# Delta net: the convolution's centre tap on ScalarE, fixed banks for projections and gate, merge chunks moved within the last head

## The reference, cut to what matters

```python
def dwconv_centred(x, w):                 # CONV_K = 4, padding 2 on the left, 1 on the right
    ...                                   # out[t] = sum over k of w[k] * x[t + k - 2], per channel
c = jax.nn.silu(dwconv_centred(qkv, conv_w))
q, k, v = jnp.split(c, [DN_QK, 2 * DN_QK], axis=-1)
q = q * rsqrt(sum(q*q) + EPS) * DN_DK ** -0.5
k = k * rsqrt(sum(k*k) + EPS)
# chunked gated delta rule, forward and backward in time:
A = where(strict, (k*beta) @ k.T * decay, 0); solve (A + I) u = v*beta, (A + I) w = k*beta*exp(gc)
v_new = u - w @ S; o = qg @ S + att @ v_new; S = S*exp(gl) + kd.T @ v_new
o = rmsnorm(o) * norm_g * silu(z)
```

## Time and profile before

| what | us |
|---|---|
| median of 3 runs (3611.55 to 3613.46) | 3612.29 |
| the profiled execution's own time | 3611.45 |
| its span in the trace | 3609.67 |
| TensorE busy (97% of the span) | 3492.7 |
| VectorE busy (52%) | 1886.8 |
| ScalarE busy (32%) | 1138.1 |
| POOL busy (24%) | 869.6 |

### The profile page before, as it was taken

How to read it: one execution, slowest core, us unless ns; L and a number is a source line. 1 busy time by engine, 2 the same in 40 slices (tenths; PEclk the granted TensorE clock), 3 DMA queues, 4 the chain that set the end, 5 groups by cost and what they waited for, 6 DMA issues and landing times.

```text
span 3609.7 us, 53450 instructions
## 1 busy us (share of the span) xinstructions
PE 3492.7 (97%) x22170; PEld 2304.4 (64%) x22170; DVE 1886.8 (52%) x3502; ACT 1138.1 (32%) x2145; POOL 869.6 (24%) x704
## 2 busy tenths in 40 slices
PE   7999999999999999999999999999999999999998
PEld 4555555665668876676666656444555545878887
DVE  3555553355445353666666653455777732554543
ACT  3443443222232022333333322764544521110100
POOL 2212121222210003444444410223445420000000
PEclk9999999999999999999999999999999999999999
DMA  5121111111102111111111111221101011322221
GB/s 227 65 79 70 56 65 47 35 35 47 35 36 105 71 65 59 48 48 39 45 48 48 54 71 59 83 76 62 48 31 48 16 64 62 112 83 81 87 81 56
DMA packets 29551, 229.73 MB, mean 64 GB/s; under 512 B 3072, under 2 KB 6784, under 8 KB 9728
## 3 DMA queue, kind: packets, MB, share of 16 engines
q1 hardware_dynamic: 29312, 226.33, 17.0%
HBM read 224.22 MB, written 2.10 MB: 63 GB/s over the span
## 4 chain that ended last, share of the span: by engine, by line
PE 88%; DVE 6%; ACT 3%; issue 1%; DMA 1%; POOL 0%; SPq 0%; DVEq 0%; ACTq 0%; POOLq 0%
PE bank L1284 12%; PE bank L1610 8%; PE bank L1503 7%; PE bank L1951 7%; PE bank L1606 4%; PE bank L1978 4%; PE bank L1730 3%; PE bank L1569 3%; PE bank L1869 2%; PE bank L1409 2%; PE bank L1689 2%; PE bank L1696 2%; PE bank L1442 2%; PE bank L1231 2%; PE bank L1915 2%
## 5 line engine op out<-in xcount | busy, mean ns | idle before, releaser
L1284 PE MATMUL bank<-xT,ring 128*128 128x384 f32 x896 | 323.4, 494 | 2.6 <-ACT Y L2093 2.4
L3606 POOL TENSOR_TENSOR ring<-ring 128x512 f32<-128x512 f32 x112 | 146.8, 1328 | 412.9 <-DMA ring<-in_w 411.2
L1284 PE MATMUL bank<-hT,ring 128*128 128x384 f32 x672 | 242.8, 493 | 0.0
L3670 POOL TENSOR_TENSOR arena<-arena 128x512 f32<-128x512 f32 x112 | 184.4, 1647 | 212.7 <-PE bank L1659 195.6
L1284 PEld LDWEIGHTS bank<-xT,ring 128*128 128x128 f32 x896 | 161.3, 190 | 108.3 <-issue 15.7
L3644 POOL TENSOR_TENSOR ring<-ring 128x512 f32<-128x512 f32 x96 | 121.3, 1268 | 282.2 <-DMA ring<-in_w 281.4
L1730 PE MATMUL bank<-hT,ring 128*128 128x512 f32 x384 | 178.9, 599 | 4.7 <-ACT Y L2068 4.7
L1610 PE MATMUL bank<-Y,ring 128*128 128x384 f32 x512 | 183.2, 497 | 0.0
L1284 PEld LDWEIGHTS bank<-hT,ring 128*128 128x128 f32 x672 | 121.4, 190 | 80.9 <-issue 16.0
L3093 DVE TENSOR_TENSOR arena<-arena 128x512 f32<-128x512 f32 x112 | 95.0, 848 | 100.8 <-PE bank L1659 99.3
L3753 POOL TENSOR_TENSOR hT<-hT,arena 128x512 f32<-128x512 f32 x3 | 5.1, 1724 | 558.6 <-ACT arena L2005 558.6
(11 more groups left out here) (590 smaller groups left out, 7587.3 us busy)
## 6 DMA issues: line engine op xcount, KB each, us to landing
ring<-in_w SPq DMA_DIRECT2D x77, 1024.0 KB, 4.8
ring<-in_w SPq DMA_DIRECT2D x35, 2048.0 KB, 7.9
ring<-in_w SPq DMA_DIRECT2D x20, 1280.0 KB, 5.5
ring<-in_w SPq DMA_DIRECT2D x10, 1536.0 KB, 6.7
ring<-in_w SPq DMA_DIRECT2D x8, 1408.0 KB, 6.0
ring<-in_w SPq DMA_DIRECT2D x6, 512.0 KB, 3.4
xT<-in_xT SPq DMA_DIRECT2D x1, 3072.0 KB, 14.6
xT<-in_xT SPq DMA_DIRECT2D x4, 512.0 KB, 7.0
```

The costliest lines, as they stand in the source:

```text
L1284: ins = e.matmul(bank[spot["st", kind, n, at]][:, 0:384], left[:, k], right[:, k], start=first and k == 0, stop=k == 3, skip_group_check=True)
L3606: e.tensor_tensor(s[:, i], l, r, op).then_inc(up("st_s", (kind, n, i)), 1)
L3670: e.tensor_tensor(o, o, gl_total(m, 1, m), ALU.mult).then_inc(up("gl_low", (j, li)), 1)
```

## The change

The change has three parts. The centre tap (tap 2, which reads the projection unshifted) is now made by ScalarE straight from the bank into dn_cv, behind the copy; VectorE adds the other three taps to it. The bank is handed on by this new instruction. The queries and values always take bank 0, the keys and the gate bank 1. In stage 7 the merge chunks are dealt out to the ticks in other numbers, 40 as before.

```diff
-MIX_AT = {..., 7: [0, 0, 3, 3, 4, 4, 4, 4, 3, 3, 3, 3, 3, 3], 8: [0, 6, 5, 5, 4] + [0] * 9}
+MIX_AT = {..., 7: [2, 1, 0, 4, 4, 4, 4, 4, 3, 3, 3, 3, 3, 2], 8: [0, 6, 5, 5, 4] + [0] * 9}
@@ tensor: def dz(j, c)
-                    take(proj, ("dz", j, 0), ("dz_silu", (j, 0)))
+                    take(1, ("dz", j, 0), ("dz_silu", (j, 0)))
@@ tensor: def dn_p(h, i, c)
-                    take(proj, ("dn_p", h, i), ("dn_padded", (h, i)))
+                    take((0, 1, 0)[i], ("dn_p", h, i), ("dn_begun", (h, i)))
@@ scalar: def dn_c(h, i)
                 e.activation(dn_pad[n % 2][:, 2:514], bank[spot["dn_p", h, i]], ACT.Copy).then_inc(up("dn_padded", (h, i)), 1)
+                if n >= 2:
+                    ph, pi = (n - 2) // 3, (n - 2) % 3
+                    q.wait_ge(*(on("dn_t_pe", (ph, 2)) if pi == 2 else on("dn_normed", (ph, pi))))
+                e.activation(dn_cv[n % 2], bank[spot["dn_p", h, i]], ACT.Copy,
+                             scale=col("dcw", 48 + 8 * i + h)).then_inc(up("dn_begun", (h, i)), 1)
@@ vector: def dn_c(h, i)
                 q.wait_ge(*on("dn_padded", (h, i)))
-                if n >= 2:
-                    ph, pi = (n - 2) // 3, (n - 2) % 3
-                    q.wait_ge(*(on("dn_t_pe", (ph, 2)) if pi == 2 else on("dn_normed", (ph, pi))))
-                e.tensor_scalar(o, c[:, 0:512], col("dcw", w), None, ALU.mult).then_inc(up("dn_conv", (h, i, 0)), 1)
-                for k in range(1, 4):
-                    q.wait_ge(*on("dn_conv", (h, i, k - 1)))
+                q.wait_ge(*on("dn_begun", (h, i)))
+                for k in (0, 1, 3):
+                    if k:
+                        q.wait_ge(*on("dn_conv", (h, i, (0, 0, 1, 1)[k])))
                     e.scalar_tensor_tensor(out=o, in0=c[:, k:k + 512], scalar=col("dcw", 24 * k + w), in1=o, op0=ALU.mult,
                                            op1=ALU.add).then_inc(up("dn_conv", (h, i, k)), 1)
```

More of the change, by code:

```diff
@@ L450, in dn_scan @@
     return made
-MIX_AT = {-1: [0, 0, 2, 2, 3, 3, 3, 3, 4, 0, 0, 0, 0, 0], 7: [0, 0, 3, 3, 4, 4, 4, 4, 3, 3, 3, 3, 3, 3], 8: [0, 6, 5, 5, 4] + [0] * 9}
+MIX_AT = {-1: [0, 0, 2, 2, 3, 3, 3, 3, 4, 0, 0, 0, 0, 0], 7: [2, 1, 0, 4, 4, 4, 4, 4, 3, 3, 3, 3, 3, 2], 8: [0, 6, 5, 5, 4] + [0] * 9}
 def dn_steps():
```

## The result

The changed kernel takes 3620.38 us (median of 12 runs, 3618.92 to 3623.33) against 3612.39 (12 runs) for the kernel before on the same chip: a ratio of 1.0022, 95% interval 1.0014 to 1.003. That is 8.0 us slower where 2.25 were forecast.

What follows compares the result with a forecast made beforehand. TensorE was taken to bound the kernel, with 88% of the chain. Stages 1 to 6 +6.3, stage 0 +0.75, stage 7 -4.8: net +2.25 on 3611.45, giving 3613.7 us (3614.5 on the median); range 3606 to 3622.

Steps and rivals of the forecast that it cites:

- The gate's stall: Gate's first chunk on TensorE waits for the keys' tap to release bank 1: +1.75 us in each of stages 1 to 6.
- The moved chunks: Stage 7: three merge chunks moved from the third tick into TensorE's idle time in the first two: -4.8 us.
- The centre tap: VectorE's convolution on the chain loses L3205: 0.7 us saved a head, seven times, bounds 0.35 and 1.45.
- Stage 0: Gate chunk starts 1.4 us later and ends 1.45 later, less 0.7 from the convolution: +0.75 us.
- Half clock after a stall: Rival: TensorE's clock falls after each new gap, about 1.7 us each; three falls give 3619.6, seven 3626; chance 0.17.
- The begin: Delta net's first projection on TensorE: the prediction's sum had no term for it.
- Bank 0 is free: TensorE's 0.78 us wait before L1730 goes, but VectorE is late there anyway: no gain.
- the new wait doesn't bite: Rival: gate chunk does not wait because ScalarE is ahead of TensorE; only gains left, -10.2, 3602 us; chance 0.14.
- the chunks bring nothing: Rival: stage 7's first two ticks become bare waits as long as before; +4.8, 3619.3 us; chance 0.07.
- The forecast's own bounds: A change of 0.2%, 7.2 us, about what measurement can tell from none: 3605.1 to 3619.5 us.

Runs made afterwards that it cites:

- e1: Changed kernel with projections and gate taking banks 0 and 1 in turn again, ScalarE tap and new chunk numbers kept; 3604.38 us.
- e4: Changed kernel with the keys' copy and tap three places earlier in ScalarE's queue, fixed banks kept; 3605.08 us.
- e8: Changed kernel with the keys' tap made twice, the bank handed on by the last; 3627.50 us.
- e3: Kernel before with the new merge chunk numbers of stage 7 alone; 3609.25 us.
- e10: Kernel before with ScalarE's tap alone, banks in turn and handed on by the tap, chunks as before; 3609.80 us.
- e11: Changed kernel with queries and values in bank 1, keys and gate in bank 0, and the keys' copy and tap three places earlier on ScalarE; 3603.66 us.
- e6: Changed kernel with banks in turn again and POOL's value scaling (dn_b) one tick earlier; 3599.37 us.
- e2: Changed kernel with the two banks exchanged: queries and values in bank 1, keys and gate in bank 0; 3618.60 us.
- e5: Kernel before with the fixed banks alone, handed on by the copy, no ScalarE tap, old chunk numbers; 3626.28 us.

## Why the prediction was right or wrong

The direction of each part was right and the sum lay 5.3 under the profile: 2.25 against 7.5. By the prediction's steps:

- **The gate's stall**, 1.55 us of gap and 1.75 a head: 1.43 to 1.52 and 1.73 (e1 less after). Right, and for the reason given: e4 takes it away by the queue's order alone, e8 lengthens it one for one.
- **The moved chunks**, -4.8: -4.85. The mechanism was right, with the clock and the uncovered wait as counted, but agreement to 0.05 is luck. From L1795 to L1815 5.0 are won, and 0.65 of them are lost again behind the third tick, where the step let the gain stay whole; 0.5 more comes with the tap, ahead of L1795, which the step did not count there. The chunks alone bring 4.33 (e3).
- **The centre tap**, 0.7 a head: 0.50 (e1, e10, e11). In the bounds, but mis-sized: 6 x 0.2 = 1.2 us. The step let all three adds run beside POOL and gave each the 1.43 to 1.44 of the earlier trace rows. POOL's timeline after shows that they do run beside it:

```profile
2615.17 1.62 POOL L3734 TENSOR_TENSOR arena<-arena,hT 128x512 f32<-128x512 f32 x1 [3.73 <-DVE arena L3284]
2616.75 1.49 POOL L3749 TENSOR_TENSOR Y<-arena 128x512 f32<-128x512 f32 x1
2618.21 1.49 POOL L3749 TENSOR_TENSOR arena<-arena 128x512 f32<-128x512 f32 x1
```

  POOL works until 2619.70, and the three L3211 end at 2620.25. The second and third took the 1.4 that was summed. The first, which stands in L3205's place beside L3734, takes 1.69 where L3205 took 1.43: that is the missing 0.2. The Trainium skill's GPSIMD Engine Reference, section Specifications, which the prediction weighed, says that VectorE instructions with two SBUF inputs contend with POOL. The runs agree: 4.67 us for three beside POOL and 2.48 clear of most of it (e6).
- **Stage 0**, +0.75: +1.35, by another way than summed. This stage begins 3.70 us later in the profile after (1.70 of lead and the begin's 2.00), so the gate's chunk starts 2534.27 - 3.70 - 2530.17 = 0.40 later than in the earlier trace rows, not 1.4, because TensorE comes to it sooner (it waits 0.82 ahead of L1803 in place of 1.60). But the whole chunk runs at half clock and takes 3.78 where the sum has the 2.95 of the earlier trace rows, and L1739 behind it 1.91 in place of 1.79: 0.40 + 0.83 + 0.12 = 1.35.

```profile
2532.07 0.42 PE L1803 MATMUL bank<-arena 32*32 32x32 f32 x29 [0.82 <-ACT arena L2463]
...
2537.84 1.91 PE L1739 MATMUL bank<-arena,cons 128*128 128x512 f32 x2
```

  The stall alone does not make this half clock. The granted clock is 0.86 on average from 2530 to 2534, so it fell before the chunk began; in e4, without the stall, the chunk still takes 3.51. In e1, with the same 0.82 ahead of L1803 and no stall, it runs at full clock:

```profile
2531.45 1.98 PE L1254 MATMUL bank<-hT,ring 128*128 128x512 f32 x4
```

  What decides it stays open.
- **Half clock after a stall**, a rival at 1.7 us each and none in the sum: one fall in the six heads, 2.89 less 1.23, about 1.65 us. The price was right. The sum had no fall in these heads, although showed one behind gaps of that size.
- **The begin**: this step failed, by being left out. "Bank 0 is free" was worked out for the steady head and stage 0, where the owner before is a projection. For the first projection of all, the owner before is the recurrence, whose gelu keeps TensorE waiting for 2.35 us. It costs 2.0 us; with the first projection in bank 1 (e2, e11) all but 0.27 of it is gone, and e5 has it without tap and chunks.

The misses add to 1.2 - 0.15 (the stall) + 0.6 + 1.65 + 2.0 - 0.05 = 5.25. The rivals that the new wait doesn't bite and that the chunks bring nothing are both ruled out, by the stall's rows and by e3's stage 7.

The measured 3620.38 lies in the stated range of 3606 to 3622, but that is luck in part: the upper end was drawn for four falls of the clock, and one came in the heads; the begin, which no rival names, and the smaller misses filled the room. The forecast's own bounds, 3605.1 to 3619.5, were passed by 0.9.

## What to carry to other kernels

A fixed buffer in place of one taken in turn changes who is the owner before at every use: go through the first use and the last as well as the steady one, and for each find where the release stands in its engine's queue. A release that stands behind an instruction which waits for the very engine that wants the buffer is a stall, and moving it up in the queue (e4) cost nothing here. What an engine saves beside another that slows it, as POOL slows VectorE here, is only worth what the other leaves of it.

## What was not expected of the hardware

- Two profiles of one kernel have a fall of the clock behind the same one of six stalls of 1.43 to 1.52 us, in stage 4 (besides stage 0), and the one that it follows, 1.43, is not the longest. The mirrored banks have it in stage 6, behind 1.44, and the double tap in stage 1, behind 2.25. Two profiles are few: a draw among six heads would hit the same head again one time in six. What singles out that head stays open.
- Contention between VectorE and POOL was moved more than removed. With dn_b earlier, L3211 x3 went from 4.67 to 2.48, but L3244 from 0.43 to 1.15 and L3245 from 0.42 to 1.27: 2.2 won, 1.6 given back, 0.96 of that out of idle time that lay between them and L3281.
